# Scores of the first cached group made one stage earlier, four queries at a time, in the space of the combined outputs

## The reference

```python
DIL_PATTERNS = ((128, 1), (512, 4), (2048, 16))      # window, dilation
for g, (window, dil) in enumerate(DIL_PATTERNS):
    qg, kg, vg = ...                                 # from x @ w_in, rotary on q and k
    ext = jnp.concatenate([cache_dil_g, new_kv], 1)  # 128 kept positions per class of the dilation
    o, lse = dilated_group_attention(qg, ext[:, :, 0], ext[:, :, 1], pos0, window, dil)
wts = jax.nn.softmax(jnp.stack(lses), axis=0)
c_out = einsum("gbhl,gblhd->blhd", wts, outs)        # the combined outputs
mq, mk, mv, ip, fp, og = parts[9:]                   # the mLSTM's projections of the same x
h, c, n, m = mlstm_chunkwise(mq, mk, mv, ip, fp, c0, n0, m0)
```

## Time and profile before

| what | us |
|---|---|
| median of 3 executions | 3887.47 |
| lowest, highest | 3878.54, 3888.53 |
| time of the profiled execution | 3891.83 |
| its span, first to last instruction | 3889.8 |
| PE busy in the span | 3569.9 |
| DVE busy | 1883.9 |
| POOL busy | 762.8 |

### The profile page before, as it was taken

How to read it: one execution, slowest core, us unless ns; L and a number is a source line. 1 busy time by engine, 2 the same in 40 slices (tenths; PEclk the granted TensorE clock), 3 DMA queues, 4 the chain that set the end, 5 groups by cost and what they waited for, 6 DMA issues and landing times. The chain is left out here.

```text
span 3889.8 us, 66425 instructions
## 1 busy us (share of the span) xinstructions
PE 3569.9 (92%) x25825; PEld 2941.6 (76%) x25825; DVE 1883.9 (48%) x2764; ACT 1169.3 (30%) x2447; POOL 762.8 (20%) x629
## 2 busy tenths in 40 slices
PE   9988888888877999999999899979887999999998
PEld 8965666666666899999998777646566899999997
DVE  2158575434367644444445365454317844444445
ACT  2156444444432121111113244331115121111112
POOL 0047222222210211111111111108311311111112
PEclk9999999999988999999999999989897999999999
DMA  3120799999803011111111210109532111111112
GB/s 135 45 51 1 316 416 415 412 413 412 350 9 124 12 44 43 43 43 43 43 43 65 74 47 31 36 27 330 200 119 73 66 44 43 43 43 43 43 43 79
DMA packets 188822, 472.84 MB, mean 122 GB/s; under 512 B 31673, under 2 KB 129845, under 8 KB 152710
## 3 DMA queue, kind: packets, MB, share of 16 engines
q1 hardware_dynamic: 168646, 449.65, 31.0%
q10 hardware_dynamic: 19936, 19.92, 1.6%
HBM read 449.61 MB, written 19.91 MB: 121 GB/s over the span
## 5 line engine op out<-in xcount | busy, mean ns | idle before, releaser
L1984 DVE TENSOR_TENSOR x<-x,f_d 128x512 f32<-128x512 f32 x540 | 368.1, 686 | 304.9 <-PE f_d L1798 249.7
L1959 POOL TENSOR_TENSOR f_hl<-f_h,f_hh 128x364 fp32r<-128x364 f32 (+1 forms) x192 | 178.4, 930 | 1255.1 <-ACT f_hh L1917 1255.1
L2004 DVE TENSOR_TENSOR f_h<-f_h 128x364 f32<-128x364 f32 (+1 forms) x192 | 105.0, 549 | 516.4 <-ACT f_h L1911 516.4
L1798 PE MATMUL f_d<-f_w2l,f_hh 128*128 128x512 f32 x896 | 354.4, 395 | 0.0
L1798 PE MATMUL f_d<-f_w2h,f_hl 128*128 128x512 f32 x896 | 354.4, 395 | 0.0
L1798 PE MATMUL f_d<-f_w2h,f_hh 128*128 128x512 f32 x896 | 354.3, 395 | 0.0
L761 DVE COPY ss_kT<-ss_tk 128x512 f32<-128x512 f32 x256 | 176.8, 692 | 327.2 <-PE ss_tk L653 211.4
L1677 PE MATMUL up<-xH,w1h 128*128 128x364 f32 (+1 forms) x768 | 255.5, 333 | 5.4 <-ACT f_h L1911 5.4
L1677 PE MATMUL up<-xL,w1h 128*128 128x364 f32 (+1 forms) x768 | 254.6, 332 | 0.0
L1677 PE MATMUL up<-xH,w1l 128*128 128x364 f32 (+1 forms) x768 | 254.4, 331 | 0.0
L1911 ACT ACTIVATE f_h<-up 128x364 f32<-128x364 f32 (+1 forms) x192 | 90.6, 473 | 540.6 <-PE up L1677 539.6
(11 more groups left out here) (598 smaller groups left out, 7863.6 us busy)
## 6 DMA issues: line engine op xcount, KB each, us to landing
ss_kv<-in_cache_sb_kv SPq DMA_DIRECT2D x336, 512.0 KB, 6.4
x<-in_cache_sb_kv SPq DMA_DIRECT2D x176, 512.0 KB, 6.3
w<-in_ffn_w SPq DMA_DIRECT2D x64, 1024.0 KB, 5.3
mp_qb<-mp_q SPq DMA_DIRECT2D x24, 1024.0 KB, 7.7
pe_raw<-in_w_in_even SPq DMA_DIRECT2D x8, 1024.0 KB, 8.2
mp_kc<-in_cache_dil_kv SPq DMA_DIRECT2D x8, 1024.0 KB, 10.4
mp_vc<-in_cache_dil_kv ACTq DMA_DIRECT2D x8, 1024.0 KB, 7.2
group_w<-in_w_in_odd SPq DMA_DIRECT2D x3, 2048.0 KB, 8.3
```

The lines of the kernel that those rows point to most:

```text
L1798: mm = pe.matmul(out, a, b, start=(n == 0), stop=(n == len(parts) - 1))
L1959: low = lambda dst, n0, n1, at: g.tensor_tensor(dst, h[:, u % HSLOTS, n0 - at:n1 - at], hh[:, c % 2, f, n0:n1].bitcast(F32), ALU.subtract)
L1984: v.tensor_tensor(K.x[0:r, t, cs], K.x[0:r, t, cs], dn_b[(c * DOWN + u) % 4][0:r, :], ALU.add).then_inc(added, 1)
L2004: v.tensor_tensor(x, x, x, ALU.mult).then_inc(squared, 1)
```

## The change

The 8 steps of the first group leave `mlstm_project` and are made in `last_prompt_and_rows`, as 16 halves of four queries. SP stores the queries to memory, then loads for each half 4 queries broadcast (512 KB) and for each sample its keys (128 KB). The two buffers of queries lie in the place of `cT`, which is written only in the next stage. POOL multiplies a half (128x1024) and then folds the 64 elements of each head to 32 by an addition into one buffer `near_f` (128x512). DVE sums the 32 into `G["s0"]`: two halves at the end of each of steps 2 to 8, and two more after the last step. In `mlstm_project` the second and third group remain (16 steps), the scores of the first group are ready at its start, and the places of all pieces among the units and in DVE's order move forward.

```diff
@@ last_prompt_and_rows
+            @block.gpsimd
+            def _(p):
+                for n in range(HALVES):
+                    b = n // 2
+                    p.wait_ge(near_q_ld[n % 2], 16 * (n // 2 + 1))
+                    p.wait_ge(near_k_ld[b % 2], 16 * (b // 2 + 1))
+                    q4 = near_b[n % 2].rearrange("p (i e) -> p i e", e=DW)
+                    p.tensor_tensor(q4, q4, near_k[:, b % 2, :].unsqueeze(1).to_broadcast([P, QH, DW]), ALU.mult).then_inc(near_mult, 1)
+                    p.wait_ge(near_mult, n + 1)
+                    if n >= 1:
+                        p.wait_ge(near_red, n)
+                    x = near_b[n % 2].rearrange("p (x d) -> p x d", d=HD)
+                    p.tensor_tensor(near_f[:, :, :], x[:, :, 0:HD // 2], x[:, :, HD // 2:HD], ALU.add).then_inc(near_fold, 1)
...
             @block.sync
+                def near(n):
+                    b = n // 2
+                    if n % 2 == 0:
+                        if b >= 2:
+                            sp.wait_ge(near_mult, 2 * (b - 1))
+                        sp.dma_start(near_k[:, b % 2, :], near_rows[b, :, 0, :]).then_inc(near_k_ld[b % 2], 16)
+                    if n >= 2:
+                        sp.wait_ge(near_fold, n - 1)
+                    src = near_q[b * DS + QH * (n % 2):b * DS + QH * (n % 2 + 1), :].rearrange("s e -> (s e)")
+                    sp.dma_start(near_b[n % 2], src.partition_broadcast(P)).then_inc(near_q_ld[n % 2], 16)
+
+                sp.dma_start(near_q, G["qs"][0][:, :]).then_inc(near_out, 16)
...
                     weights.start(sp)
+                    sp.wait_ge(near_out, 16)
+                    for n in range(2):
+                        near(n)
                     next_weights.start(sp)
+                    for n in range(2, HALVES):
+                        near(n)
                     sp.wait_ge(st, 1)
...
             @block.vector
+                def reduce_near(count):
+                    for n in range(reduced[0], reduced[0] + count):
+                        v.wait_ge(near_fold, n + 1)
+                        v.tensor_reduce(G["s0"][:, n // 2, QH * (n % 2):QH * (n % 2 + 1), :].rearrange("p i h -> p (i h)"), near_f[:, :, :],
+                                        AX.X, ALU.add).then_inc(near_red, 1)
+                    reduced[0] += count
                 for t in range(NTL + 1):
...
                     if t in between:
                         between[t]()
+                    if t >= 2:
+                        reduce_near(2)
+                reduce_near(HALVES - reduced[0])
                 keep_columns()
@@ mlstm_project
-    NKV = 3 * DB
+    NKV = 2 * DB
-    scores_at, turn_at, new_at, collect_at = [14, 23, 34], [18, 27, 42], [19, 28, 43], [23, 34, 53]
-    value_units = [19, 20, 21, 22, 28, 30, 31, 33, 43, 46, 49, 52]
+    scores_at, turn_at, new_at, collect_at = [3, 14, 26], [5, 18, 31], [6, 19, 32], [14, 26, 45]
+    value_units = [7, 8, 9, 10, 19, 20, 22, 24, 32, 36, 40, 44]
...
-                for w in range(4):
+                for w in range(3):
                     for b in range(DB):
                         n = DB * w + b
-                        if w >= 2 and b == 0:
-                            mask_heads(w - 2)
-                        if w >= 1 and b == 1:
-                            centre(w - 1)
-                        if w >= 2 and b == 2:
-                            finish(w - 2)
-                        if w >= 1 and b == 3:
-                            scale(w - 1)
-                        if w >= 1 and b == 4:
-                            log_sum(w - 1)
+                        if w >= 1 and b == 0:
+                            mask_heads(w - 1)
+                        if b == 1:
+                            centre(w)
+                        if w >= 1 and b == 2:
+                            finish(w - 1)
+                        if b == 3:
+                            scale(w)
+                        if b == 4:
+                            log_sum(w)
                         if n < NKV:
                             reduce(n)
```

More of the change, by code:

```diff
@@ L2615, in last_prompt_and_rows @@
         keys_done, keys_kept, KEYS = K.sem("mk_dn"), K.sem("mk_kp"), 6
+        HALVES, QH = 2 * DB, DS // 2
+        near_rows = io["cache_dil0_kv"][0].rearrange("b n s h d -> b n s (h d)")
+        near_q = nc.dram_tensor("mp_q0", (NSMP, DW), F32, kind="Internal").ap()
+        near_k = sb("nk", [P, 2, DW])
+        near_b = [nc.alloc_sbuf_tensor_at(f"dl_nb{i}", [P, QH * DW], F32, offset=G["cT_at"] + 4 * QH * DW * i)[:, :] for i in range(2)]
+        near_f = sb("nf", [P, QH * DILH, HD // 2])
+        near_out, near_mult, near_fold, near_red = (K.sem("dl_n" + n) for n in ("o", "m", "f", "r"))
+        near_k_ld, near_q_ld = ([K.sem(f"dl_n{n}{i}") for i in range(2)] for n in ("kl", "ql"))
         dv_at = {"decayed": DECAYED}
@@ L3048, in mlstm_project @@
     NK = P + NSMP
-    NKV = 3 * DB
+    NKV = 2 * DB
     per_class = [min(WINDOWS[g][1], DS) for g in groups]
     rows = [io[f"cache_dil{g}_kv"][0].rearrange("b (n r) s h d -> b n r s (h d)", r=WINDOWS[g][1]) for g in groups]
-    scratch = [nc.dram_tensor(f"mp_q{g}", (NSMP, DW), F32, kind="Internal").ap() for g in groups]
-    scores_at, turn_at, new_at, collect_at = [14, 23, 34], [18, 27, 42], [19, 28, 43], [23, 34, 53]
-    value_units = [19, 20, 21, 22, 28, 30, 31, 33, 43, 46, 49, 52]
+    scratch = [None] + [nc.dram_tensor(f"mp_q{g}", (NSMP, DW), F32, kind="Internal").ap() for g in (1, 2)]
+    scores_at, turn_at, new_at, collect_at = [3, 14, 26], [5, 18, 31], [6, 19, 32], [14, 26, 45]
+    value_units = [7, 8, 9, 10, 19, 20, 22, 24, 32, 36, 40, 44]
     SETS = 3
@@ L3102, in keys @@
                 def keys(n):
-                    g, b = divmod(n, DB)
+                    g, b = 1 + n // DB, n % DB
                     c = per_class[g]
@@ L3108, in keys @@
                     if b == 0:
-                        sp.wait_ge(q_out, 16 * 3)
+                        sp.wait_ge(q_out, 16 * 2)
                     if n >= SETS:
@@ L3115, in _ @@
                 for g in groups:
-                    sp.dma_start(scratch[g], G["qs"][g][:, :]).then_inc(q_out, 16)
+                    if g >= 1:
+                        sp.dma_start(scratch[g], G["qs"][g][:, :]).then_inc(q_out, 16)
                     sp.dma_start(mask[:, g, :], io["c_dmask"][g]).then_inc(mask_ld, 16)
@@ L3135, in _ @@
                 for n in range(NKV):
-                    g, b = divmod(n, DB)
+                    g = 1 + n // DB
                     p.wait_ge(k_ld[n % SETS], 16 * (n // SETS + 1))
@@ L3181, in scores @@
                         pe.matmul(n_b[h % 2][:, h // 2, :], qk[lo:lo + HD, h // 2, :], qk[lo:lo + HD, 2 + h // 2, :], start=True, stop=True)
-                    pe.wait_ge(red, DB * (g + 1))
+                    if g >= 1:
+                        pe.wait_ge(red, DB * g)
                     for h in range(DILH):
-                        mm = pe.transpose(c_b[:, slot(h), :], s_[:, g % 2, :, :, h].rearrange("p b i -> p (b i)"), K.ident[:, :])
+                        mm = pe.transpose(c_b[:, slot(h), :], s_[g % 2][:, :, :, h].rearrange("p b i -> p (b i)"), K.ident[:, :])
                     mm.then_inc(raw, 1)
@@ L3342, in reduce @@
                 def reduce(n):
-                    g, b = divmod(n, DB)
+                    g, b = 1 + n // DB, n % DB
                     v.wait_ge(mult, n + 1)
-                    v.tensor_reduce(s_[:, g % 2, b].rearrange("p i h -> p (i h)"), qb[n % SETS].rearrange("p (x d) -> p x d", d=HD),
+                    if g == 2 and b == 0:
+                        v.wait_ge(raw, 1)
+                    v.tensor_reduce(s_[g % 2][:, b].rearrange("p i h -> p (i h)"), qb[n % SETS].rearrange("p (x d) -> p x d", d=HD),
                                     AX.X, ALU.add).then_inc(red, 1)
@@ L3896, in program @@
             G["cT"] = odd.enter_context(nc.sbuf_tensor("cT", [P, 2, NT], F32, side="right"))
+            G["cT_at"] = nc._sbuf_addr_for_side("right")
+            G["s0"] = odd.enter_context(nc.sbuf_tensor("s0", [P, DB, DS, DILH], F32, side="right"))
             w_keys = io["w_in_odd"][0].rearrange("(k p) n -> p k n", p=P)[:, :, MC0 + MW:MC0 + 2 * MW]
```

3 lines of the change are left out of this document (2 added, 1 removed).

## The result

The changed kernel takes **3924.17 us** (median of 4, 3922.95 to 3924.94) where the kernel before takes 3888.0 (3878.54 to 3889.36): a ratio of 1.0091 with a 95% interval of 1.0079 to 1.0103, so it is slower by 36 us. The forecast was 3912, slower by 25, in a range of 3884 to 3934.

The account below looks back on a forecast made before the run. PE, busy 92% of the span, was taken as the bound, so its gaps and clock decide. First stage +16 us and second stage +9 us on 3887.5 gave 3912 us, range 3884 to 3934.

Parts of the forecast that it names:

- The pairs: First stage: DVE waits for POOL's second fold, 2.8 us of its queue per step; steps 5 to 7 give +5.7.
- The lock: First stage, steps 5 to 8: DVE operations with two SBUF inputs held by POOL through the shared port, 4 us.
- The tail: End of first stage: the last pair's load, product, fold and reduction, of which 2 us show.
- The removal: Second stage: 8 products and 8 reductions with their loads taken out, by itself worth nothing.
- The first softmax: Second stage: PE waits 10 us where it waited 2.07, behind three second-group reductions; +8.5 with slower clock.
- Values of the first group: Second stage: three load intervals of 8.8 us hold 10.5 us of units instead of 15; +4.5.
- Values of the second and third group: Second stage: waits of 3.5 us, then 5.3 and 2.5; net -8.5 for the second group, +12 for the third.
- the clock terms: Second stage: slower PE matmuls after waits, such as 1 us at the first softmax and 1.8 per value wait.
- ACT's copies: Second stage: third-group exponentials no longer stand among key copies; -4.71 us of wait and 2.6 of clock, -7.3.
- The value loads land within their units: Rival, chance 0.17: second-stage value loads land in 4 to 5 us, that stage gives -17, the whole 3887.
- The first stage hides everything: Rival, chance 0.13: PE does not feel the pairs, only the second stage counts, the whole 3896.
- The lock is the price: Rival, chance 0.17: DVE pays up to 2.26 us, three times per step; +27 and +16 by stage, 3930.

Follow-up runs that it names:

- e5: e3 with POOL's products and folds cut to an eighth of the elements, loads and DVE's reductions unchanged: 3913.12 us, first stage 99.1 us.
- e1: The changed kernel with the second stage's places and DVE's order put back to those of the kernel before: 3909.22 us, second stage 268.3 us.
- e3: The changed kernel with a second buffer for near_f, so a pair's second fold need not wait for DVE: 3923.32 us, first stage 110.3 us.
- e6: The changed kernel with three query buffers, folds in place and DVE's reductions moved into its waits for ACT: 3930.54 us, first stage 120.9 us.
- e11: The kernel before with only its places in the second stage spread, without the move: 3867.26 us, ratio 0.9940.
- e2: The changed kernel without the first group's products, reductions and loads in the first stage (scores set to zero): 3906.20 us, first stage 95.2 us.

## Why the prediction was right, and where it was off

The sign and both mechanisms were right, and the time lay in the range; the size was 12 us short. Within the first stage two errors of opposite sign partly cancelled, so that its 16 us look better than its terms. By its own steps:

- **The pairs** (8.5 us: 2.8 of the early 4.4, and 5.7 for steps 5 to 7) were costed too high. DVE waited 1.43 to 1.45 us for POOL before each second reduction of steps 2 to 7, as forecast. Up to the last logarithm, DVE's queue holds twelve reductions (8.7 us) and six such waits (8.6), less 11.5 us of its waits for ACT that took them up: 5.8.
- **The lock** (4 us, and 1.6 in the early steps: 5.6) is the term that was mis-sized. Six normalisations (L2787) took 4.4 us more than 0.69 each, four of the small additions (L2792) 6.1 more than 0.16, L2780 0.4: 10.9. I had counted operations of 0.69 us, "that last 1.5 to 2.5"; they lasted 1.3 and once 2.0, and the dearest were those of four columns, which were overlooked, though each of them may stand for all that is left of a POOL instruction. e5 shows it in time, 11.2 us with the tail's part. Pairs and lock together, 16.7 us, stand against 15.8 by which DVE's queue from its first operation to its last logarithm grew (2512.51 to 2569.91 before, 2511.64 to 2584.88 after).
- **The tail** (2 us): the copy of columns came 14.3 us after the last logarithm for 11.8, 2.5 us.
- **The removal** of products and reductions from the second stage was put at nothing; e1 against the kernel before shows 4.9 us less.
- **The first softmax** (a wait of 10): 9.67, with some luck. POOL's first product came 14.8 us after the stage's first matmul, 1.4 earlier than reckoned, and the hold was 4.2 us, 1.2 longer. (The prediction's own terms give +8.9 for this step, not +8.5.) The step held was `centre(0)`'s last, 5.13 us for 0.95, in this row of DVE's timeline:

```profile
2660.09 5.13 DVE L3414 TENSOR_TENSOR mp_z<-mp_z,mp_m 64x768 f32<-64x768 f32 x1
```

- **Values of the first group** (+4.5): waits of 2.59, 3.26 and 7.11 us, 13.0 for 8.5, so +4.5. But the three are unlike, and I had them equal. From 2688 to 2709 us the loads took 8.9 us to land, with a DMA share of 1.02 and 355 GB/s:

```profile
mp_vc<-in_cache_dil_kv ACTq DMA_DIRECT2D x4, 128.0 KB, 8.9
```

- **Values of the second and third group** (waits of 3.5 and of 7.8): 6.6 and 9.6. These 4.9 us are most of what the second stage's +9 lacked to 13.4; the clock terms, small in the sum, came out at nothing, since PE's busy time in the stage is unchanged (240.65 and 240.81).
- **ACT's copies** (-4.71): the wait is gone, as forecast.
- **The states**: not foreseen at all, +2.8. One DVE operation of one column took 4.18 us there (its longest before was 1.19, though the one ahead of it then took up to 1.95 and now 0.73), behind three POOL instructions in a row; DVE's and POOL's timelines after:

```profile
2938.76 4.18 DVE L3738 TENSOR_TENSOR mc_den<-mc_den,cols 128x1 f32<-128x1 f32 x1
```

```profile
2938.56 1.93 POOL L3692 TENSOR_TENSOR ms_kwm<-kn,ms_wsm 64x1024 f32<-64x1024 f32 x1
2940.46 2.47 POOL L3678 TENSOR_TENSOR mc_Mall<-mc_Mall,mc_mask 128x512 f32<-128x512 f32 x2
```

The code is the same in both kernels, and the other profiles show that the stage's length goes with these holds. In the four kernels whose longest held operation there stayed under 2 us (before, e3, e6, e11) the stage took 102.4 to 103.5 us; in the nine others, where it was 2.4 to 4.2 us, it took 104.9 to 107.5. e3 and e6 have the move and are among the four, so the growth does not come with the move every time. Why DVE and POOL meet differently from kernel to kernel is open; no run was made for it.

**The rivals.** *The value loads land within their units* fell with 29.2 us of waits. *The first stage hides everything* fell with e2. *The lock is the price* was right in its kind and too dear: it gave 3930 and wanted +27 in the first stage, which grew by 18.8. It had three operations in a step at up to 2.26 us each. Three in a step did meet a busy POOL, but they lost 0.1 us, mostly 0.6 (once 1.3), and up to 1.8 in four of seven cases, since little was left of POOL's instruction when they came. By the Trainium skill (SBUF — State Buffer, the section on two separate sides) the one of the two engines that comes second is blocked fully until the other's instruction is over. The trace agrees: the small addition ended at 2564.00 us and POOL's product at 2563.98.

What the forecast left out is that its two terms are not of one kind. The first stage's 19 us are the price of the move as it is made here. The second stage's 13 are the price of a list of numbers: with other numbers the same move ends at 3877, and with other numbers the kernel before, without it, at 3867.

## What to carry to other kernels

When a change moves work and re-times the rest, run the old kernel with only the timing redone: here that alone gave 23 us, and the best kernel with the move was 6.5 slower than that. Work put on an idle POOL beside a DVE that the critical engine waits for should be priced by what is left of a POOL instruction for each two-input DVE operation that meets it, tiny ones above all. And a second buffer gives less than the waits that it removes where the engine that it sets free runs straight into that lock: here 3.6 us of the stage, for six waits of 1.44.

## What the runs showed of the hardware

- In these rows a DVE operation that was held ended with POOL's instruction or up to 0.8 us behind it, so what it lost went by what was left of that instruction and not by its own size. Two operations of 128x4 and 128x1 (0.16 us alone) took 1.96 and 4.18 us and ended with POOL's instruction; the 64x768 subtraction of 0.95 us took 5.13 and ended 0.8 us behind the product that held it, which ended at 2664.41.
- The 4.18 us end at 2942.94, the last of three POOL instructions queued back to back at 2942.93; DVE did not get in between them. It is not always so: an addition of 64x4 (L3425) held 3.79 us from 2672.80 ended at 2676.59, with the first of four products of 4.5 us in a row.
- The hold also met a COPY of 4x7 (2.28 us for 0.16) and a scan of 4x1088 (3.36 for 2.41), both in e6. Operations that take one of two inputs from PSUM (L2776 at 0.69) and reductions (L2860 at 0.69) kept their times beside a busy POOL.
- POOL is held in its turn: 2.80 us for 2.36, 1.60 for 1.26.
- Value loads of 128 KB took 8.9 us to land in a stretch where the DMA engines moved 355 GB/s, while 512 KB took 5.0 us with the queues nearly empty.
